# Seven block products instead of eight in a feed-forward input product, with the residual spilled unscaled

## The reference, cut to what matters

```
x = first_block(...)                       # ends with rms_norm(x, final_g)
h = rms_norm_2(x, mix_pre_g) * (1 + sc1) + sh1
y = hybrid_mixer(h, ...)                   # attention and a causal depthwise convolution of 31 taps
x = x + g1 * rms_norm_2(y, mix_post_g)
h = rms_norm_2(x, ffn_pre_g) * (1 + sc2) + sh2
g, u = split(h @ w_ffn_in)                 # 1024 x 1024 times 1024 x 5632: the first FFN product
y = (silu(g) * u) @ w_ffn_out              # 1024 x 2816 times 2816 x 1024: the second
x = x + g2 * rms_norm_2(y, ffn_post_g)     # g2 comes from the modulation vector number 11
```

## Time and profile before

| | |
|---|---|
| median of 3 runs | 2404.48 us (2403.85 to 2405.51) |
| the profiled execution's own time | 2405.95 us |
| its span | 2404.2 us |
| granted TensorE clock, mean | 0.976 |
| PE busy | 2267.9 us, 94% |
| POOL busy / DVE busy / ACT busy | 1404.4 / 1475.4 / 774.9 us |

### The profile page before, as it was taken

The page is one execution under the profiler, slowest core; times in us unless marked ns, Lnnn a source line. Parts: engine busy times, 40 slices in busy tenths (PEclk is TensorE's granted clock), DMA queues, the critical chain, the costliest instruction groups (busy, mean ns, idle before and its releaser), DMA issues. The chain is left out here.

```text
span 2404.2 us, 32299 instructions
## 1 busy us (share of the span) xinstructions
PE 2267.9 (94%) x11283; PEld 1887.9 (79%) x11283; DVE 1475.4 (61%) x2169; ACT 774.9 (32%) x1394; POOL 1404.4 (58%) x1359
## 2 busy tenths in 40 slices
PE   5999999999999999999979988899999999999995
PEld 3888889888888878877758867787888888888874
DVE  4835646587893999968899879747512222222236
ACT  4320113123121888833434267733210000000012
POOL 2555557565975888467898544376746433333360
PEclk8999999999999999999989989999999999999997
DMA  9345454424566665352243665442323211111121
GB/s 339 119 135 175 124 158 147 161 67 153 175 194 188 184 176 158 97 202 80 70 138 110 192 166 158 129 171 90 95 63 93 73 53 53 53 45 45 52 70 70
DMA packets 181039, 301.74 MB, mean 126 GB/s; under 512 B 34764, under 2 KB 73352, under 8 KB 179856
## 3 DMA queue, kind: packets, MB, share of 16 engines
q1 hardware_dynamic: 147120, 219.60, 32.1%
q10 hardware_dynamic: 33760, 80.07, 9.0%
HBM read 245.05 MB, written 54.56 MB: 125 GB/s over the span
## 5 line engine op out<-in xcount | busy, mean ns | idle before, releaser
L1215 PE MATMUL PS<-HXH,WH 128*128 128x512 f32 x1888 | 746.4, 395 | 33.1 <-ACT TM L1967 15.0
L1095 POOL TENSOR_SCALAR WH<-RAW 128x512 fp32r<-128x512 f32 x458 | 341.6, 746 | 704.4 <-PE PS L1217 553.6
L1216 PE MATMUL PS<-HXL,WH 128*128 128x512 f32 x1888 | 739.1, 391 | 0.0
L1217 PE MATMUL PS<-HXH,WL 128*128 128x512 f32 x1888 | 739.0, 391 | 0.0
L1098 POOL TENSOR_TENSOR WL<-RAW,WH 128x512 fp32r<-128x512 f32 x458 | 637.4, 1392 | 38.2
L1215 PEld LDWEIGHTS PS<-HXH,WH 128*128 128x128 f32 x1888 | 357.4, 189 | 115.9 <-POOL WL L1098 8.4
L1216 PEld LDWEIGHTS PS<-HXL,WH 128*128 128x128 f32 x1888 | 357.4, 189 | 74.9 <-issue 1.9
L1217 PEld LDWEIGHTS PS<-HXH,WL 128*128 128x128 f32 x1888 | 356.8, 189 | 75.5
L2622 DVE TENSOR_TENSOR TM<-PS,TM 128x512 f32<-128x512 f32 x44 | 29.3, 691 | 344.8 <-ACT TM L1998 339.1
L1998 ACT ACTIVATE TM<-PS 128x512 f32<-128x512 f32 x44 | 26.0, 598 | 534.5 <-PE PS L1217 533.4
L2635 DVE TENSOR_TENSOR Y<-PS,Y 128x2048 f32<-128x2048 f32 x40 | 91.7, 2292 | 117.5 <-PE PS L1217 115.4
(11 more groups left out here) (330 smaller groups left out, 4142.4 us busy)
## 6 DMA issues: line engine op xcount, KB each, us to landing
RAW<-in_ada_w SPq DMA_DIRECT2D x160, 256.0 KB, 2.9
RAW<-in_w_ffn_in SPq DMA_DIRECT2D x224, 128.0 KB, 2.1
RAW<-in_w_in_ab SPq DMA_DIRECT2D x88, 256.0 KB, 2.7
RAW<-in_w_in SPq DMA_DIRECT2D x56, 256.0 KB, 2.7
RAW<-in_w_ffn_out SPq DMA_DIRECT2D x56, 256.0 KB, 2.7
XX<-XR ACTq DMA_DIRECT2D x3, 4096.0 KB, 14.8
RAW<-in_w_in_c SPq DMA_DIRECT2D x40, 256.0 KB, 2.7
EARLY<-in_ada_w SPq DMA_DIRECT2D x32, 256.0 KB, 9.3
```

Of the source, the lines that this page charges most:

```text
L1095: g.tensor_scalar(WH[:, sw, 0:m], RAW[:, r, 0:m], 1.0, 0.0, ALU.mult, ALU.add).then_inc(gpsimd_done, 1)
L1215: mm(out, wh, xh, start=first, stop=False, **kw)
L1216: mm(out, wh, xl, start=False, stop=False, **kw)
L1217: return mm(out, wl, xh, start=False, stop=last, **kw)
```

## The change

**Seven products.** In the chunks 2 to 9 the input product is done in 16 pages of 128 hidden columns. A page's product is a 2x2 block product: rows `h0` and `h1`, inner halves (tiles 0 to 3 and 4 to 7), columns of g and of u. It uses seven block products of 4 x 3 = 12 matmuls instead of eight: 84 a page instead of 96. The factors are A11, A12, A22 and the sums S1 to S4 of the four weight blocks (POOL makes 4 sums a page, ACT all seven H parts, POOL all seven L parts, in 4 slots), and on the other side the input's own tiles and four sums T1 to T4 of them.

**The sums T.** The steps `tk` 0 to 3 make T1, T2 and T4 (7 sums, 3 L parts on DVE, 3 H parts on ACT each), two ahead of `fi 0 h1` and two ahead of `fi 1 h1`. The steps `t3` 0 to 3 make T3 (3 sums and an L part), one behind each `fo` of the chunks 0 and 1 for `h1`. They write where X and half of the input lie. So X is spilled a third time (`spill 3`, 4 MB, issued by ACT behind the squares of `sum 4 h1`), two blocks of the input are stored (`b12out`, 2 MB), and all is read back behind the pages (`reload 3`). 

**Vector 11.** Its `adapool` is moved ahead, in two halves: 8 tiles behind the splits of `fi 0 h1`, 8 behind those of `fi 1 h1` and `fo 0 h1`. The last L part of `tk 3` waits for all 16, because its place is the scratch tile that they use.

**X.** The step `xw` is moved from ahead of `cv h1` to ahead of the projection `(wo, 1, h0)`, and waits there for the reload; `conv -3` now stands ahead of `flogz`; the spill takes X as it is.

**The start.** `stat 0 h0` is moved ahead of the squares of `h1`.

```
-    ev("sum", ("sum", 0, "h1"), n=0, part="h1")
     ev("stat", ("stat", 0, "h0"), n=0, part="h0")
+    ev("sum", ("sum", 0, "h1"), n=0, part="h1")
...
         if (name, p) == ("cv", "h1"):
-            for x in x2:
-                ev("xw", ("xw", x), part=x)
+            ev("conv", ("conv", -3), i=-3)
             ev("flogz", "flogz")
-            ev("conv", ("conv", -3), i=-3)
...
+        if (g, p) == (1, "h0"):
+            for x in x2:
+                ev("xw", ("xw", x), part=x)
...
     ev("sum", ("sum", 4, "h1"), n=4, part="h1")
+    ev("spill", ("spill", 3), n=3)
...
+    ev("b12out", "b12out")
+    w = weights("fi", 0)
+    ada_half(0)
+    ev("tk", ("tk", 0), k=0)
+    ev("tk", ("tk", 1), k=1)
+    hidden(0, "h1", w)
+    w = weights("fi", 1)
+    ws = [out_weights(0)]
+    ada_half(1)
+    ev("tk", ("tk", 2), k=2)
+    ev("tk", ("tk", 3), k=3)
+    hidden(1, "h1", w)
+    ws.append(out_weights(1))
+    for x in range(4):
+        if x == 3:
+            ev("adapost", ("adapost", 11, None), v=11, n=None)
+        lin(("fo", x // 2, x % 2, "h1"), "fo", x % 2, "h1", ws[x // 2][x % 2], kts=2, last=True, h="A", ch=x // 2,
+            midk=1, mid=("adac", 11, None) if x == 3 else None)
+        ev("t3", ("t3", x), k=x)
...
+    ev("pages", "pages", blocks=blocks, outs=outs)
+    ev("reload", ("reload", 3), n=3)
```

On DVE, a `tk` step and the wait in it:

```
+                        step(x1, f32("h1", k, 0), f32("h0", k, 0), ALU.subtract, ("T1a", k))
...
+                        t_lows(2, x2)
+                        if k == 3:
+                            dve.wait_ge(*of("ada_acc", 11, None, KT - 1, 1))
+                        t_lows(4, x4)
```

On PE, the pages; the output products of the chunk before stand between the seven units of every second page (`OUT_AT`):

```
+                    for pg in range(PAGES):
+                        for i in range(7):
+                            page_product(pg, i)
+                            if pg % 2 == 0 and pg:
+                                for f in OUT_AT[i]:
+                                    page_out(e, PAGE_CH[pg // 2 - 1], f)
+                    for f in range(8):
+                        page_out(e, PAGE_CH[-1], f)
```

On POOL, a page:

```
+                    combine(pg, "S3", block(pg, "A21"), block(pg, "A11"), block(pg, "A21"), ALU.subtract)
+                    combine(pg, "S2", SRAW[:, :], block(pg, "A22"), block(pg, "A21"), ALU.subtract)
+                    low(pg, 0)
+                    combine(pg, "S1", block(pg, "A11"), SRAW[:, :], block(pg, "A11"), ALU.add)
+                    low(pg, 1)
+                    low(pg, 2)
+                    combine(pg, "S4", block(pg, "A12"), block(pg, "A12"), SRAW[:, :], ALU.subtract)
+                    if outs:
+                        split(outs[0])
+                    low(pg, 3)
+                    if outs:
+                        split(outs[1])
+                    for i in range(4, 7):
+                        low(pg, i)
```

More of the change, by code:

```diff
@@ L136, in plan @@
     ev("txc", "txc")
+    ev("stat", ("stat", 0, "h0"), n=0, part="h0")
     ev("sum", ("sum", 0, "h1"), n=0, part="h1")
-    ev("stat", ("stat", 0, "h0"), n=0, part="h0")
     ev("adac", ("adac", 0), v=0)
@@ L389, in plan, with ada_half @@
         hidden_out(x // 2, "h0", ws[x // 2], gs=(x % 2,))
[L390 to L404, removed]
+    ev("b12out", "b12out")
+    def ada_half(half):
+        tiles = [(11, k, x, slot("raw", ("ada", 11, k, x), None)) for k in range(4 * half, 4 * half + 4) for x in range(2)]
+        ev("adapool", ("adapool", 11, half), ada=tiles, after=("H", "apply", 4, "h1", KT - 1))
+    w = weights("fi", 0)
[16 more added lines that the diff above has]
+        ev("t3", ("t3", x), k=x)
+    blocks, outs = {}, {}
+    for pg in range(PAGES):
+        ch, x = PAGE_CH[pg // 2], pg % 2
+        for which in ("A11", "A21", "A22", "A12"):
+            blocks[pg, which] = slot("block", ("fiw", (ch, x, which), None), None)
+        if x == 1 or ch > PAGE_CH[0]:
+            c_, g = (ch, 0) if x else (ch - 1, 1)
+            for k in range(2):
+                outs[c_, g, k] = slot("outs", ("fo", (c_, g), k), None)
+    for k in range(2):
+        outs[PAGE_CH[-1], 1, k] = slot("outs", ("fo", (PAGE_CH[-1], 1), k), None)
+    ev("pages", "pages", blocks=blocks, outs=outs)
+    ev("reload", ("reload", 3), n=3)
     hidden(nch - 1, "h0", weights("fi", nch - 1))
@@ L732, in program @@
                     order.append((e["mid"], e))
-            if e["kind"] in ("attc", "attf") or (e["kind"] == "conv" and e["i"] == -3):
+            if e["kind"] in ("attc", "attf", "pages") or (e["kind"] == "conv" and e["i"] == -3):
                 order.append((e["name"], e))
@@ L747, in program @@
                 cur, only = 1 - only, None
+                continue
+            if e["kind"] == "pages":
+                outset = cur = 1 - cur
+                setof["pages"], setof["pages_out"] = 1 - outset, outset
+                prev["pages"], prev["pages_out"] = [lastin[1 - outset]], [lastin[outset]]
+                lastin = {1 - outset: "pages", outset: "pages_out"}
+                cur = 1 - outset
                 continue
@@ L1135, in _ @@
             for e in TL:
+                if e["kind"] == "pages":
+                    split_until(page_slots[0])
+                    page_weights(e)
+                    done[0] = page_slots[-1] + 1
                 if e["kind"] == "conv":
@@ new lines, in page_out @@
+            def page_out(e, ch, f):
+                g, p, jp = OUT_UNITS[f]
+                if f < 2 and ch > PAGE_CH[0]:
+                    pe.wait_ge(*of("yadd2", ch - 1, 6 + f))
+                elif f < 2:
+                    for job_before in prev["pages_out"]:
+                        pe.wait_ge(*of("free", job_before))
+                else:
+                    pe.wait_ge(*of("yadd2", ch, f - 2))
+                for k in range(2):
+                    n = e["outs"][ch, g, k]
+                    pe.wait_ge(gpsimd_done, upto("w", n))
+                    pe.wait_ge(vector_done, upto("A", ch, p, k))
+                    c0 = PARTS[p][0]
+                    for j in range(2):
+                        ws = slice((2 * jp + j) * P, (2 * jp + j + 1) * P)
+                        ins = three(bank("pages_out", 2 * (f % 2) + j), WH[:, WPOS[n], ws], WL[:, WPOS[n], ws],
+                                    AHH[:, k, c0:c0 + HALF], AHL[:, k, c0:c0 + HALF], k == 0, k == 1)
+                ins.then_inc(products_done, 1)
+                did(products_done, ("fou", ch, g, p, jp))
@@ L1288, in _ @@
             for e in TL:
                 kind, name = e["kind"], e["name"]
+                if kind == "pages":
+                    for pg in range(PAGES):
+                        for i in range(7):
[5 more added lines that the diff above has]
+                        page_out(e, PAGE_CH[-1], f)
+                    continue
```

352 lines of the change are left out of this document (325 added, 27 removed).

## The result

The changed kernel took 2411.58 us (median of 6 runs, 2408.55 to 2413.44), the kernel before in the same job 2403.98 (2399.25 to 2405.51): ratio 1.0036, 95% interval 1.0026 to 1.0046, so 8.7 us slower by the ratio (6 to 11) and 7.6 by the two medians. I had 2401 as the likeliest and gave "slower" 0.28. The profiled execution of the changed kernel took 2408.55, the shortest of its six; the one before, 2405.95, lay 2 over its median.

A forecast was written before the change was run, and what follows sets the result against it. PE, busy 94% of the span, was taken as the bound. From 2404.48 us, -43.5 (pages) + 42 (T) - 12.7 (convolution) + 14.5 (wo stage) - 3.5 (start) = -3.2 gave 2401 us, range 2373 to 2416.

The forecast's parts named there:

- The pages: 16 pages with 12 matmuls fewer each, at 0.227 us a matmul and with no PE wait: -43.5 us.
- rivals 2 and 4: POOL paces the short pages, +12 (2413); or 12 matmuls into one bank may not keep 2.72 us; together 0.13.
- the T term: Sums T and vector 11, up to page 0: +40 us, +42 with PE's half clock after the wait.
- (a) to (d): T section: POOL's vector 11 tiles; DVE contention, POOL ends 1779; fo (0,1) waits till 1781.4; t3 chain, page 0 at 1809.5.
- Rival 1: DVE and POOL hardly meet, so T costs 25 us and xw 1: 2371, half way 2386; chance 0.29.
- Rival 3: T section: DVE and POOL exclude each other wholly, +27 us for POOL, vector 11 ready at 1792: 2414; chance 0.13.
- The start: First layer: ada 1 starts about 5 us earlier, modulation comes at 50 instead of 53.6: -3.5 us, bounds 0 and -5.
- X in the convolution: xw leaves DVE's list ahead of flogz, PE's gate-bank waits shrink: -12.7 us, bounds -7 (POOL's taps) to -19.
- X in the wo stage: xw on DVE delays the row sum of stat 3 h0: +14.5 us, other bound +1; 1.46 us a multiplication.

The follow-up runs named there:

- e4: The changed kernel with 14 of the 16 tiles of vector 11 left out: 2387.49 us, 0.9943 of the kernel before.
- e6: The changed kernel with tk 3 behind fi 1 h1 and the H parts of page 0's first two units behind t3 1: 2399.62 us, 0.9992 of before.
- e1: The kernel before with only stat 0 h0 moved ahead of the h1 squares: 2402.31 us, 1.0003 of before.
- e10: The changed kernel with sum 0 h1 behind apply 0 h0 and the row sum stat 0 h1 inside xb h0: 2410.68 us, 1.0035 of before.
- e2: The kernel before with only the X part of the change, no pages or T sums: 2408.51 us, 1.0027 of before.
- e3: The changed kernel with xw in halves, h0 ahead of (wo,1,h0) and h1 ahead of (wo,1,h1): 2407.09 us, 1.0025 of before.
- e8: The changed kernel with the h1 half of xw behind normed h0 of the wo stage: 2405.80 us, 1.0022 of before.
- e7: The changed kernel with vector 11 made beside the attention and the order edits of e6: 2390.85 us, 0.9954 of before.
- e9: The changed kernel with its X part undone: 2402.52 us, 1.0002 of before.
- e11: The changed kernel with e7, e8 and e10 together and vector 11's row sums read in the last fo of h0: 2388.56 us, 0.9940 of before.

## Why the prediction was wrong

- *The pages*: right. No wait, 0.227 a matmul in blocks of 12, so rivals 2 and 4 fall. -41.5 for -43.5: the 2 us are the half clock in the first 12 matmuls of page 0 (4.86 us for 2.72), which I had put into the T term. With them moved there the pages are -43.6 for -43.5.
- *(a) to (d), the T section*: right as a mechanism, in its order and in its size, 41.4 up to page 0 for 40, and 43.5 with the half clock behind the wait for 42: POOL's end at 1782.26, against 1779 on a clock that was by then 2.6 us behind; one wait of 21.03 released by DVE, one of 7.87 behind ACT and POOL. e4 takes the cause away and the wait goes by half; e6 shows that the place of tk 3 alone only moves it. The wait of 4.31 at fi 1 h1 I had missed; it was covered. Rival 1 falls, since DVE and POOL did meet: beside POOL's splits a tk took 13.1 (I had 13.5), alone 7.1. Rival 3 falls by its own mark, POOL's end, which was not later than 1787.
- *The start*: the step "stat 0 h0 no longer stands behind 8 squares, so `ada 1` starts about 5 us earlier ... the modulation comes at 50" fails. ada 1 did, but "ACT then has the squares ahead of its copy" was the smaller part; I did not ask what stands between adac 0 and adac 1: DVE's MOD of the first was now behind the sums. +0.3 for -3.5, and +0.5 in e1, which has this step alone. e10 shows that even a gain of 6 there is worth under 1 at 220 us.
- *X in the convolution*: mis-sized, and for a wait that I did not look for. I asked what is late next at the gate banks, and there the -12.7 was nearly right (-10.6, and -12.2 in e2). I did not ask it again at q2's banks, where ACT's copies stand behind taps that POOL paces: 5 of it goes. -5.2 for -12.7; the bound of -7 that I had named for POOL's taps was not low enough, in this profile or in the six later ones with -6.4 to -6.5.
- *X in the wo stage*: the step was right in its place and its chain, +11.5 for +14.5: the reload was there in time, a multiplication took 1.24 to 1.32 us instead of 1.46.

So X is +6.3 where I had +1.8, the start +0.3 where I had -3.5, and T and the pages -0.1 together where I had -1.5: 9.7 us off, all of it optimistic. These are differences within one pair of profiles, and by e2 and the spread of the convolution stage X's own +6.3 can be 3 us less. The two terms that are large in themselves were right to 5%; the sign was decided by small ones, of which each was costed at its first stop.

## What to carry to other kernels

A gain in time at one point is to be followed through the next two or three waits, with every list that it passes: e10 gave back 5 of 6 us, X in the convolution 5 of 10, and a wait taken out of the wo stage came back 40 to 50 us later in e3 and e8. Where one engine's list holds both a long wait for a slow helper and the operation that frees a bank, either move the helper's work to a stage in which it has room or the bank's operation ahead; here each alone gave 10.6 us, both 20 (e7), and both with X taken out and the start mended turned a loss of 9 us into a gain of 17. And a move onto a list that has room for half of the work pays the other half, wherever it is put.

## What the runs showed of the hardware

*The granted clock after one short wait differs between executions.* PE waits 3.2 to 3.9 us for MOD at 1085 in all kernels. Windows of all engines as above, behind that wait, in the kernel before, in the changed kernel, and in e9:

```profile
1088.00:1090.00 2.00, 2.00 (x6) 1.58 (x5) 1.93 (x3) 1.19 (x2) 0.00 (x1) 0.50 0.00 0
```

```profile
1088.00:1090.00 2.00, 2.00 (x10) 1.65 (x10) 1.95 (x3) 1.25 (x3) 1.09 (x2) 1.00 0.15 55
```

```profile
1088.00:1090.00 2.00, 2.00 (x6) 1.58 (x5) 1.97 (x4) 1.76 (x3) 0.00 (x0) 0.50 0.38 127
```

In the first and third PE ran at 0.50, 1.2 GHz, and lost 3 us to the second, which stayed at 1.00 (2.4 GHz) through the same wait. The profiles of the changed kernel, e6 and e10 show the good case, those of the kernel before and of nine others the bad one, and e11 one between. It is 3 of the 6 us by which the changed kernel's profile looks better, against before's, than the runs (2.5 for 8.7). A difference of 3 us between two single profiles is to be looked for in such spots before it is explained.

*Two engines at once.* Ten operations of DVE took 13.04 us beside POOL's splits and 7.1 without, in one trace (e4). The Trainium skill (SBUF — State Buffer, section Who interferes with whom) lets the later of the two wait for the other's whole length. The traces agree that they hold each other up, and not that it is for the whole of the times shown: with that rule, worked out as the third rival, I had POOL's end at 1792, and it was 1782. Which part of an instruction's time is shut out no run here isolates.
